# Front projections of a hybrid attention block with activations stationary, and the turns through memory that this asks for

## The reference, cut to what matters

```python
xn   = rmsnorm(x, attn_norm)
proj = xn @ w_in            # 512 cq | 256 ckv | 64 kr | 1024 fq | 1024 fk | 1024 fv | 8 ff | 4096 gates
cq   = rmsnorm(proj[cq], q_norm);  q  = cq @ w_uq      # 8 heads, 128 nope + 64 rope
ckv  = rmsnorm(proj[ckv], kv_norm); kv = ckv @ w_ukv   # 8 heads, 128 keys + 128 values
k    = [kv keys, apply_rope(proj[kr])]; q = [q nope, apply_rope(q rope)]
o_mla = attention(q, k, kv values, chunk mask)          # scale 1/sqrt(192)
cum  = cumsum(log_sigmoid(proj[ff] + f_bias))
o_fox = attention(fq, fk, fv, causal, bias cum[t] - cum[s])
h = x + (sigmoid(gates_a) * (o_mla @ w_mla) + sigmoid(gates_b) * (o_fox @ w_fox)) @ w_out
u = relu(rmsnorm(h, mlp_norm) @ w_up) ** 2
y = rmsnorm(h + u @ w_down, final_norm)
```

## Time and profile before

| | us |
|---|---|
| median of 3 runs | 1292.23 (1292.09 to 1293.36) |
| the profiled execution | 1292.3, of it 1290.2 span |
| PE busy | 1281.5 (99%) |
| DVE busy | 754.0 (58%) |
| ACT busy | 601.7 (47%) |
| POOL busy | 104.6 (8%) |
| granted clock of PE, mean | 0.999 |

### The profile page before, as it was taken

One profiled execution on the slowest core, in us unless ns is written; L12 is line 12 of the kernel. 1 busy time (PEld: TensorE's weight loads), 2 busy tenths in 40 slices (PEclk: granted clock), 3 DMA queues, 4 the chain that ended last, 5 costly groups with the idle time before them and its releaser, 6 DMA issues.

```text
span 1290.2 us, 14677 instructions
## 1 busy us (share of the span) xinstructions
PE 1281.5 (99%) x5896; PEld 1069.8 (83%) x5896; DVE 754.0 (58%) x766; ACT 601.7 (47%) x697; POOL 104.6 (8%) x170
## 2 busy tenths in 40 slices
PE   9999999999999999999999999999999999999997
PEld 8888888888888888888888888888888888888886
DVE  6676566645666667666565664444455656554543
ACT  6645444545555445445454544333344444453443
POOL 0100001100221111110101010000001101100000
PEclk9999999999999999999999999999999999999999
DMA  8656648666656788785878776666668787766653
GB/s 321 243 192 200 213 160 245 192 215 189 189 175 205 209 279 259 225 250 199 245 240 251 236 244 207 191 193 194 195 212 243 241 242 238 251 204 211 195 194 117
DMA packets 78404, 280.65 MB, mean 218 GB/s; under 512 B 10232, under 2 KB 10752, under 8 KB 77696
## 3 DMA queue, kind: packets, MB, share of 16 engines
q1 hardware_dynamic: 67104, 243.04, 59.0%
q0 software_dynamic: 10224, 34.63, 8.7%
q10 hardware_dynamic: 1008, 2.05, 0.5%
HBM read 262.89 MB, written 16.79 MB: 217 GB/s over the span
## 4 chain that ended last, share of the span: by engine, by line
PE 99%; DVE 0%; ACT 0%; DVEq 0%; POOL 0%; issue 0%; ACTq 0%; POOLq 0%
PE bank L646 28%; PE bank L648 28%; PE bank L647 28%; PE bank L566 8%; PE bank L571 4%; PE bank L712 1%; PE bank L747 1%; PE bank L697 0%; PE bank L698 0%; PE bank L695 0%; PE bank L715 0%; PE bank L731 0%; PE bank L551 0%; DVE resid L1427 0%; DVE final L1436 0%; ACT square L1055 0%
## 5 line engine op out<-in xcount | busy, mean ns | idle before, releaser
L1099 DVE TENSOR_TENSOR hl<-raw,hl 128x1024 fp32r<-128x1024 f32 x455 | 554.6, 1226 | 476.1 <-ACT hl L869 475.3
L869 ACT ACTIVATE hl<-raw 128x1024 fp32r<-128x1024 f32 x455 | 479.0, 1058 | 587.8 <-PE bank L648 527.3
L646 PE MATMUL bank<-hl,hn_hl 128*128 128x512 f32 x512 | 199.3, 389 | 0.0
L648 PE MATMUL bank<-hl,hn_hl 128*128 128x512 f32 x512 | 199.3, 389 | 0.0
L647 PE MATMUL bank<-hl,hn_hl 128*128 128x512 f32 x512 | 199.2, 389 | 0.0
L646 PE MATMUL bank<-hl,u_hl 128*128 128x512 f32 x512 | 199.2, 389 | 0.0
L648 PE MATMUL bank<-hl,u_hl 128*128 128x512 f32 x512 | 199.2, 389 | 0.0
L647 PE MATMUL bank<-hl,u_hl 128*128 128x512 f32 x512 | 199.2, 389 | 0.0
L646 PE MATMUL bank<-hl,x_hl 128*128 128x512 f32 x320 | 126.2, 394 | 0.0
L648 PE MATMUL bank<-hl,x_hl 128*128 128x512 f32 x320 | 124.7, 390 | 0.0
L647 PE MATMUL bank<-hl,x_hl 128*128 128x512 f32 x320 | 124.6, 389 | 0.0
(11 more groups left out here) (193 smaller groups left out, 1172.4 us busy)
## 6 DMA issues: line engine op xcount, KB each, us to landing
raw<-weights SPq DMA_DIRECT2D x455, 512.0 KB, 4.3
turn_rows<-blocks POOLq DMA_DIRECT2D x22, 512.0 KB, 3.6
turned<-turn_rows POOLq DMA_DIRECT2D x88, 128.0 KB, 4.7
prob_rows<-prob_blocks POOLq DMA_DIRECT2D x8, 384.0 KB, 2.8
prob_t<-prob_rows POOLq DMA_DIRECT2D x32, 96.0 KB, 5.4
x_rows<-x_n POOLq DMA_DIRECT2D x2, 1024.0 KB, 11.3
resid<-x_n POOLq DMA_DIRECT2D x1, 2048.0 KB, 8.4
x_in<-x_t SPq DMA_DIRECT2D x3, 512.0 KB, 8.1
```

What stands on the lines that cost most here:

```text
L646: nc.tensor.matmul(ps, tile[:, k, 0, tok], high, start=k == 0, stop=False)
L648: return nc.tensor.matmul(ps, tile[:, k, 1, tok], high, start=False, stop=k == WIDE_SLABS * gr.units - 1)
L869: nc.scalar.activation(hl[:, slot, 0], raw[:, slot], ACT.Copy).then_inc(unit_hi, 1)
L1099: nc.vector.tensor_tensor(hl[:, slot, 1], raw[:, slot], hl[:, slot, 0].bitcast(F32), ALU.subtract).then_inc(unit_split, 1)
```

## The change

All groups now have activations stationary. cq is one group of 8 units; ckv, kr and ff become one group `keys` of 328 columns in 6 units of three slabs (the last of one). cq, keys, fq, fk, uq_nope, uq_rope and the keys of ukv are turned through memory, eleven tiles, and so are the last chunks of m and h. Norms are scaled by rows, out of PSUM. The rotation of the rotary key moves to POOL and, like that of the queries, is done with tokens on partitions, before the turn. The two groups behind a turn (w_out 0 and 1, up0 0 and 1) run side by side: six units of each, and then two of each. The first group starts on its high half before the low one is there, behind 5 warm-up products. Behind fq's first unit, `DUE` places the new steps: norms, the turn of the keys, and what follows from them.

```diff
-SLABS, COLS = 4, 256
-WIDE_SLABS, WIDE = 2, 512
+SLABS, WIDE = 2, 512
+KEY_SLABS, KEYS = 3, KV_LORA + ROPE + HEADS
 RING = 4
-WARM_UPS = 9
+WARM_UPS = 5
+AHEAD = 6
...
+    add("cq", 0, KT)
+    add("keys", 0, KT, 4, KEY_SLABS, KEYS)
+    for name in ("fq", "fk", "fv"):
+        for g in range(HEADS * DH // WIDE):
+            add(name, g, KT)
...
+    add("uq_nope", 0, KQ, 4)
+    add("uq_nope", 1, KQ, 6)
+    add("gates", 5, KT, this)
+    add("uq_rope", 0, KQ, 4)
+    add("ukv_k", 0, KKV, other)
+    add("ukv_v", 0, KKV, 6)
+    add("gates", 6, KT, this)
+    add("ukv_k", 1, KKV, other)
+    add("ukv_v", 1, KKV, 6)
+    add("gates", 7, KT, this)
...
+    def side_by_side(name):
+        add(name, 0, KT)
+        add(name, 1, KT)
+        one, two = groups[-2:]
+        one.unit = one.unit[:AHEAD] + [u + AHEAD for u in one.unit[AHEAD:]]
+        two.unit = [u for u in range(one.u0, two.last + 1) if u not in one.unit]
+        one.last, two.u0 = one.unit[-1], two.unit[0]
...
+TURNED = [("cq", 0), ("keys", 0), ("fq", 0), ("fq", 1), ("fk", 0), ("fk", 1),
+          ("uq_nope", 0), ("uq_nope", 1), ("ukv_k", 0), ("uq_rope", 0), ("ukv_k", 1)]
+TURNED += [("y_mla", g) for g in range(CHUNKS)] + [("w_out", g) for g in range(CHUNKS)]
...
-        if gr.name == "w_out" and gr.g == 0:
-            after(TURN_M, "m turned", CHUNKS - 1)
-        elif gr.name == "up0" and gr.g == 0:
-            after(TURN_H, "h turned", CHUNKS - 1)
+        if gr.name in ("y_mla", "w_out") or gr.name[:2] == "up":
+            after(gr.last + TURN_UNITS, {"y": "m turned", "w": "h turned", "u": "u turned"}[gr.name[0]], gr)
+        if gr.name == "fq" and gr.g == 0:
+            for later, what in ((0, "x norm"), (1, "latent norms"), (3, "keys rotated"), (8, "cq turned"),
+                                (10, "keys turned"), (12, "forget exp"), (13, "forget sums")):
+                after(gr.u0 + later, what, gr)
...
+        elif gr.name in ("fq", "uq_nope"):
+            after(gr.last + 6, "queries turned", gr)
+        elif gr.name == "uq_rope":
+            after(gr.last + 4, "queries rotated", gr)
+            after(gr.last + 9, "queries turned", gr)
...
+            pool.wait_ge(unit_split, BY["cq", 0].last + 1)
...
+            def take_turn(key, back, tiles=4):
+                n, run = TURN_NO[key], tiles * TB * 32
+                pool.wait_ge(blocks_turned, n + 1)
+                pool.dma_start(turn_rows[n % 2, :, 0:4 * run], blocks[:, 0:4 * run]).then_inc(blocks_stored, 16)
+                pool.wait_ge(blocks_stored, 16 * (n + 1))
+                if n:
+                    pool.wait_ge(turned_in, 4 * 16 * n)
+                if key in QUERIES and QUERIES.index(key):
+                    pool.wait_ge(queries_copied, QUERIES.index(key))
+                for q in range(4):
+                    pool.dma_start(back[32 * q:32 * q + 32].rearrange("p a k b j -> p a (k b j)"),
+                                   turn_rows[n % 2, :, run * q:run * q + run].rearrange("(a p) e -> p a e", a=4)
+                                   ).then_inc(turned_in, 16)
...
+            def rotate(z, t, cos, sin):
+                half = ROPE // 2
+                then_wait(nc.gpsimd.tensor_tensor(t[:, :, 0:half], z[:, :, half:], sin[:, :, 0:half], ALU.mult))
+                then_wait(nc.gpsimd.tensor_tensor(t[:, :, half:], z[:, :, 0:half], sin[:, :, half:], ALU.mult))
+                then_wait(nc.gpsimd.tensor_tensor(z, z, cos, ALU.mult))
+                return nc.gpsimd.tensor_tensor(z, z, t, ALU.add)
...
+            take_turn(("cq", 0), turned_q)
+            pool.wait_ge(consts_in, 16)
+            pool.wait_ge(token_out, BY["keys", 0].n + 1)
+            rotate(key_rows[:, :, KV_LORA:KV_LORA + ROPE], rope_t[:, 0:TB], cos, sin).then_inc(keys_rotated, 1)
+            take_turn(("keys", 0), turned_k, KEY_TILES)
+            for g in range(2):
+                take_turn(("fq", g), turned_h)
+            take_turn(("fk", 0), fk[:, 0])
...
+                take_turn(("uq_nope", g), turned_h)
+            pool.wait_ge(token_out, BY["uq_rope", 0].n + 1)
+            for tb in range(TB):
+                one = lambda table: table[:, tb].unsqueeze(1).broadcast_to([P, HEADS, ROPE])
+                rotate(query_rows[:, tb], rope_t[:], one(cos), one(sin)).then_inc(queries_rotated, 1)
+                pool.wait_ge(queries_rotated, tb + 1)
+            take_turn(("ukv_k", 0), kn[:, 0])
+            take_turn(("uq_rope", 0), turned_h)
+            take_turn(("ukv_k", 1), kn[:, 1])
...
+            def product(gr, tile, i, s, tb, x_part, w_part):
+                k = gr.slabs * i + s
+                w = hl[:, slot_of(gr.unit[i]), w_part, gr.cols * s:gr.cols * s + gr.cols]
+                return nc.tensor.matmul(bank[:, gr.pair + tb, 0:gr.cols], tile[:, k, x_part, tb * P:tb * P + P], w,
+                                        start=k == 0 and not x_part and not w_part,
+                                        stop=k == gr.tiles - 1 and x_part == 1)
...
+                        if k == 0:
+                            pe.wait_ge(first_hi, 1)
+                        else:
+                            pe.wait_ge(unit_hi, u + 1)
+                        pe.wait_ge(x_hi, k + 1)
+                        for tb in range(TB):
+                            product(gr, tile, i, s, tb, 0, 0)
...
+            def side_by_side(name, tile, ready):
+                one, two = BY[name, 0], BY[name, 1]
+                for gr in (one, two):
+                    wait_for_banks(gr)
+                    token_units(gr, tile, last=AHEAD, before_unit=ready)
+                for gr in (one, two):
+                    token_units(gr, tile, first=AHEAD, before_unit=ready)
...
+            first_group(BY["cq", 0], x_hl)
+            token_group(BY["keys", 0], x_hl)
+            for name in ("fq", "fk", "fv"):
+                for g in range(2):
+                    token_group(BY[name, g], x_hl)
...
+            def squares(gr, i, cols):
+                act.wait_ge(unit_used, gr.last + 1)
+                for tb in range(TB):
+                    nc.scalar.activation(square[:, tb, 0:cols], bank[:, gr.pair + tb, 0:cols], ACT.Square,
+                                         accum_out=latent_sq[:, i, tb:tb + 1]).then_inc(latents_squared, 1)
...
+            def latent_norms():
+                x_col = rstd_col[:, X_NORM]
+                dve.wait_ge(latents_squared, 2 * TB)
+                for i, d in enumerate((Q_LORA, KV_LORA)):
+                    ins = nc.vector.scalar_tensor_tensor(mean_qkv[:, i], latent_sq[:, i], 1.0 / d, x_col,
+                                                         ALU.mult, ALU.mult)
...
+            def take_latents():
+                queries, keys = BY["cq", 0], BY["keys", 0]
+                scale_rows(full, queries.pair, slice(0, Q_LORA), rstd_col[:, Q_NORM]).then_inc(token_out, 1)
+                dve.wait_ge(zeroed, 2)
+                scale_rows(key_rows[:, :, 0:KV_LORA], keys.pair, slice(0, KV_LORA), rstd_col[:, KV_NORM])
+                scale_rows(key_rows[:, :, KV_LORA:KEYS], keys.pair, slice(KV_LORA, KEYS),
+                           rstd_col[:, X_NORM]).then_inc(token_out, 1)
+                dve.wait_ge(token_out, queries.n + 1)
+                turn_blocks(queries, full[:])
...
+                elif gr.name in ("fq", "fk", "uq_nope", "ukv_k"):
+                    dve.wait_ge(blocks_turned, turns[0])
+                    if gr.name[0] == "f":
+                        ins = scale_rows(full, gr.pair, slice(0, WIDE), x_col_fox if gr.name == "fq" else rstd_col[:, X_NORM])
+                    elif gr.name == "uq_nope":
+                        ins = nc.vector.tensor_scalar(full[:], both, MLA_SCALE, None, ALU.mult)
+                    else:
+                        ins = nc.vector.tensor_copy(full[:], both)
+                    ins.then_inc(token_out, 1)
+                    dve.wait_ge(token_out, gr.n + 1)
+                    turn_blocks(gr, full[:])
+                elif gr.name == "uq_rope":
+                    nc.vector.tensor_scalar(query_rows[:].rearrange("p b h r -> p b (h r)"), both, MLA_SCALE, None,
+                                            ALU.mult).then_inc(token_out, 1)
...
+                    elif what == "x norm":
+                        reciprocal_rms(X_NORM)
+                        dve.wait_ge(rstd_col_done, X_NORM + 1)
+                        then_wait(nc.vector.tensor_scalar(x_col_fox[:], rstd_col[:, X_NORM], FOX_SCALE, None, ALU.mult))
+                    elif what == "latent norms":
+                        latent_norms()
+                        take_latents()
+                    elif what == "keys rotated":
+                        dve.wait_ge(keys_rotated, 1)
+                        turn_blocks(BY["keys", 0], key_rows[:], KEY_TILES)
+                    elif what == "cq turned":
+                        turned_to_lo(BY["cq", 0])
+                    elif what == "keys turned":
+                        turned_to_lo(BY["keys", 0])
```

(31 more changed lines are left out.)

750 lines of the change are left out of this document (226 added, 524 removed).

## The result

Seven executions took 1294.32 to 1299.28 us, median **1297.08**; as many of the kernel before 1291.85 to 1293.36, median 1292.28. The ratio is 1.0034, 95% interval 1.0021 to 1.0047: slower, by 4.8 us between the medians (4.4 by the ratio), where 1285.9 was forecast. The executions also spread more, 5.0 us against 1.5. The mean granted clock of each was recorded: 0.997 and 0.996 in those of 1294.3 and 1295.0, 0.995 and 0.994 in those of 1299.0 and 1299.3.

What follows compares the result with a forecast made beforehand. TensorE was taken to bound the kernel, holding 99% of the chain of waits. From 1292.3 us, 10.3 of gains and 3.9 of stalls gave 1285.9 us, range 1281.5 to 1290.0.

Steps and rivals of the forecast that it cites:

- keys: ckv and krff as 96 products of 328 columns, 0.147 us each: 14.1 us instead of 16.81, gain 2.7.
- fq and fk: From 47.26 to 138.02, 90.76 us before; 384 products at 0.2267 us take 87.05: gain 3.7.
- last chunks of m and h: No longer transposed on TensorE, 0.8 us twice, and the first product behind each 0.09 late before: gain 1.75.
- unit 14: Wanted at 42.9 instead of 47.3, split ending at 43.5, pulled in by earlier x rows: 0 (0 to 0.6).
- unit 22: VectorE waits for POOL's rotated keys; split at 67.4, TensorE wants it at 64.7: stall 2.7, bounds 0 and 7.6.
- unit 29: VectorE's gains, low halves and small operations make its split 0.5 late: stall 0.5 (0 to 1.5).
- rotary queries: POOL's rotation and stores delay unit 124's split and uq_rope's copy before the scores: stall 0.7 (0 to 5).
- rival without stalls: The waits on POOL are absorbed by the lead of four units: 1282.0 us, chance 20%.
- layout's pace: Measured 0.2267 us a product, activations stationary, gives the layout some 3.5 us; the skill's rule gives some 0.5.
- The clock: Rival: TensorE falls to half clock in the stall at unit 22, 2.5 us lost: 1288.4, chance 8%.
- slower rival: POOL waits 7.9 us for stores; stalls of 7.6 at unit 22, some 12 at unit 124 and scores: 1302, chance 5%.
- lowest sum: Whole kernel with no stall and keys at the low bound: 1281.5 us, the lower end of the range.

Runs made afterwards that it cites:

- c1_best: Changed kernel with uq_rope computed earlier, x rows fetched later in two pieces, rotated keys and their followers, fq and uq_nope 1 turns later: 1281.94 us.

## Why the prediction was wrong, point by point

The changed kernel's profiled execution against the steps of the prediction (the gains are differences of starts against the earlier trace rows; spacing is taken out of the waits):

| step | forecast | measured |
|---|---|---|
| start and cq | -1.65 | -1.44: cq ends 29.01 |
| keys | -2.7 | -2.46: 0.1495 us a product |
| fq and fk | -3.7 | -3.5 |
| uq and ukv_k | -0.5 | -0.5 |
| last chunks of m and h | -1.75 | -1.7 |
| unit 14 | 0 | +1.5 |
| unit 22 | +2.7 | +2.9 |
| unit 29 | +0.5 | 0 |
| rotary queries: unit 124 | +0.2 | +1.65 |
| rotary queries: scores | +0.5 | +4.7 |
| clock behind the scores' wait | (rival, at unit 22) | +1.7 |
| w_out | 0 | +0.3 |
| sum | -6.4 | +3.2; span +3.2 |

- **The gains were right**: 9.6 of 10.3 us. The best proof is `c1_best`: it keeps every product of the change, waits nowhere from unit 1 on, and takes 1281.94, where the rival without stalls had 1282.0; that the two agree to 0.1 is luck, since the gains fell 0.7 short. For the keys, the line through the two old widths (0.149) was nearer than the proportion.
- **The layout's pace**, 0.2267 us a product, held in fq and fk (384 products, -3.5 us). The Trainium skill's rule (TensorE: Matmul & The Clock Gate, "Wait — 56ns, not 53.3ns?"), which gave the layout only 0.5 us, is not borne out by them: it has 0.216 us.
- **Unit 14** failed at "I take 0 (0 to 0.6)". I had seen that the fetch moved one unit earlier and thought that it helped. In the profiled execution ScalarE waited longer for the weights before it, had unit 14 at 42.52 instead of 41.17, and the split ended 1.3 us later than the 43.5 forecast. The wait comes and goes between profiles with this fetch, so why it came in this one is only in part known.
- **Unit 22** was right in mechanism, place and size: 2.9 for 2.7. The chain started 2.5 us later than put (POOL's store at 59.94 for 57.4) and TensorE wanted the unit 2.1 us later, so the difference nearly stood.
- **The rotary queries** failed, the term with most weight: 0.7 forecast, 6.4 measured, over the upper bound of 5. The rotation's length (12 us) and the landing of ukv_k 0's store were right. Two other steps were not. "Rotation begins at 3.6": it began at 5.3 behind the end of unit 115, since VectorE scales the queries behind the split of unit 119, and these 1.7 us are the wait at unit 124. And "ScalarE waits for uq_rope until some 32.4": it was 37.8, by the same 1.7 us, by uq_rope's own store, 6.79 us where the chain has room for some 3.5, and by its last load, 5.7 us where 4.7 were put. The mean of 3.5 us came from stores with free time before them; this one was bound to stand right behind the loads of ukv_k 0. Of eleven front turns of the changed kernel, POOL waited 5.7 to 6.5 us for the stores of four (two of them placed so), and 2.6 to 4.6 for the others.
- **The clock** was a rival at 8%, at unit 22. It fell, but at the scores in the profiled execution, and at units 14, 22 or 34, or at m, in other kernels. Without it the profiled execution would stand at some 1293.5, still outside the range; with it the time varies: median and profiled execution stood 0.1 apart in the sum, and are 1.9 apart now.
- **The slower rival** (1302, at 5%) had slow landings, POOL's queue held through them, as the cause at both places. At the scores that was so, at unit 22 it was not: the store there kept POOL waiting 2.84 us. The stalls came to 11.1 us in the profiled execution, 12.8 with the slow clock, near the 13 from which that rival was to decide.
- The lowest sum of the shown terms is 1281.8 and not 1281.5; nothing hangs on it. Of the signs named: fv started at 135.1 for 133, the pace held, the scores had 4.7 us before them for under 1, and w_out showed a gap, of 0.17 us of idle time.

## What to carry to other kernels

A turn through memory has a round trip of varying length; ask for it late enough for the longest seen, not the mean, and check at the other end that its consumer does not come first. Look whether a store will be issued right behind loads of the same queue: such stores landed late every time. Moving a bulk fetch earlier can cost where a ring of weights refills. And a wait of TensorE can cost its own length and then 1.7 to 3 us of half clock behind it: where a wait cannot be removed, cheap products in it pay.
